# Two hand-overs and the first tiles of layer two: the order of VectorE's splits and of SyncE's loads in a decoder step

## What is computed

```python
def _sq_relu_mlp(x, w1, w2):                 # w1: 1024 x 4096, w2: 4096 x 1024
    return jnp.square(jax.nn.relu(x @ w1)) @ w2
...
for l in range(DEPTH):                       # DEPTH = 2
    ...                                      # l = 0: attention, l = 1: pooling mixer
    xp = xp + _rms(mp, gl[1])
    xp = xp + _rms(_sq_relu_mlp(_rms(xp, gl[2]), mlp_w1[l], mlp_w2[l]), gl[3])
```

## Time and profile before

| | |
|---|---|
| median of three runs | 2125.13 us |
| the profiled execution, its own time | 2128.65 us |
| its span in the profile | 2126.9 us |
| TensorE (PE) busy | 2048.9 us, 96% of the span |
| VectorE (DVE) busy | 1310.8 us, 62% |
| ScalarE (ACT) busy | 922.2 us, 43% |
| GpSimd (POOL) busy | 356.8 us, 17% |
| mean granted TensorE clock | 0.986 of full |

### The profile page before, as it was taken

One profiled execution on the slowest core, in us unless ns is written; L12 is line 12 of the kernel. 1 busy time (PEld: TensorE's weight loads), 2 busy tenths in 40 slices (PEclk: granted clock), 3 DMA queues, 4 the chain that ended last, 5 costly groups with the idle time before them and its releaser, 6 DMA issues.

```text
span 2126.9 us, 34612 instructions
## 1 busy us (share of the span) xinstructions
PE 2048.9 (96%) x13923; PEld 1837.2 (86%) x13923; DVE 1310.8 (62%) x1888; ACT 922.2 (43%) x1591; POOL 356.8 (17%) x375
## 2 busy tenths in 40 slices
PE   7999999999999999999899999989999998999998
PEld 7999877777778899999788878889999997888876
DVE  5121187666556778787645467669687776444475
ACT  5111397645445444444333346454444444333343
POOL 1000131000053333331000013222232320000011
PEclk9999999999999999999999999999999999999999
DMA  5321211099522577777876542444677769664464
GB/s 168 96 74 51 101 70 35 1 355 366 160 97 84 203 260 244 258 246 285 299 252 228 165 159 97 132 135 141 208 256 243 252 223 341 230 223 160 159 221 139
DMA packets 206235, 394.39 MB, mean 185 GB/s; under 512 B 19005, under 2 KB 101109, under 8 KB 197756
## 3 DMA queue, kind: packets, MB, share of 16 engines
q1 hardware_dynamic: 199884, 387.46, 53.4%
q10 hardware_dynamic: 6192, 4.72, 0.7%
HBM read 273.12 MB, written 119.24 MB: 184 GB/s over the span
## 4 chain that ended last, share of the span: by engine, by line
PE 64%; DMA 6%; DVE 5%; POOL 2%; issue 2%; SPq 1%; ACT 1%; POOLq 0%; DVEq 0%; ACTq 0%
PE ps L1957 26%; PE ps L2604 25%; PE ps L4135 4%; PE ps L1975 3%; PE ps L1918 2%; DMA sa_vb_even<-cache_b_v 1%; DMA sa_vb_odd<-cache_b_v 1%; PE ps L4055 1%; DMA l_b_raw<-scratch_t_ops 1%; PE ps L1927 1%; SPq L675 1%; PE ps L4028 1%; DVE l_t_sum L2892 1%; DMA wo_raw<-attn_w_out 1%; DMA l_w_raw<-mlp_w 1%
## 5 line engine op out<-in xcount | busy, mean ns | idle before, releaser
L1957 PE MATMUL ps<-t_b_hi,t_a_hi 128*128 128x512 f32 x448 | 178.2, 398 | 7.3 <-DVE t_b_lo L1751 6.3
L1957 PE MATMUL ps<-l_b_hi,l_a_hi 128*128 128x512 f32 x448 | 175.7, 392 | 8.0 <-DVE l_b_lo L1751 7.0
L1957 PE MATMUL ps<-t_b_lo,t_a_hi 128*128 128x512 f32 x448 | 175.4, 391 | 0.0
L1957 PE MATMUL ps<-t_b_hi,t_a_lo 128*128 128x512 f32 x448 | 175.3, 391 | 0.0
L1957 PE MATMUL ps<-l_b_lo,l_a_hi 128*128 128x512 f32 x448 | 175.2, 391 | 0.0
L1957 PE MATMUL ps<-l_b_hi,l_a_lo 128*128 128x512 f32 x448 | 175.2, 391 | 0.0
L1530 POOL TENSOR_SCALAR stats<-stats 128x1 f32<-128x1 f32 x63 | 32.6, 518 | 785.7 <-ACT t_junk_y L1524 611.0
L1748 DVE TENSOR_TENSOR l_a_lo<-l_a_raw,l_a_hi 128x1024 fp32r<-128x1024 f32 x56 | 68.6, 1225 | 144.3 <-ACT l_a_hi L2634 144.3
L2634 ACT ACTIVATE l_a_hi<-l_a_raw 128x1024 fp32r<-128x1024 f32 x56 | 59.4, 1061 | 219.0 <-PE ps L1975 140.0
L1748 DVE TENSOR_TENSOR t_a_lo<-t_a_raw,t_a_hi 128x1024 fp32r<-128x1024 f32 x56 | 68.6, 1224 | 133.7 <-ACT t_a_hi L2634 133.7
L2634 ACT ACTIVATE t_a_hi<-t_a_raw 128x1024 fp32r<-128x1024 f32 x56 | 59.4, 1061 | 195.8 <-PE ps L1975 135.7
(11 more groups left out here) (390 smaller groups left out, 5693.3 us busy)
## 6 DMA issues: line engine op xcount, KB each, us to landing
scratch_s_ops<-u_s SPq DMA_DIRECT2D x16, 1280.0 KB, 4.8
scratch_t_ops<-u_t SPq DMA_DIRECT2D x16, 1280.0 KB, 5.7
t_a_raw<-scratch_s_ops SPq DMA_DIRECT2D x40, 512.0 KB, 3.9
t_b_raw<-scratch_t_ops SPq DMA_DIRECT2D x40, 512.0 KB, 4.8
scratch_t_ops<-l_t SPq DMA_DIRECT2D x16, 1280.0 KB, 5.5
scratch_s_ops<-l_s SPq DMA_DIRECT2D x16, 1280.0 KB, 4.6
l_a_raw<-scratch_s_ops SPq DMA_DIRECT2D x40, 512.0 KB, 3.9
l_b_raw<-scratch_t_ops SPq DMA_DIRECT2D x40, 512.0 KB, 4.8
```

Of the source, the lines that this page charges most:

```text
L1957: mm = self.nc.tensor.matmul(self.core.ps[:, self.BANK[idx] + tp, :], a[s][:, kk, tp * P:(tp + 1) * P], w[s][:, kk, :], start=(c == 0 and ...
```

## The change

Three edits. In both `up_loads`, `load_operands(3)` is issued before `load_w2(15)` and no longer after it. In `SevenUp.dve_up`, which `LateUp` uses too, VectorE splits operand 2 before `combine_t(15)` and no longer after it, so the loops of both down products start at 3. In `LateUp`, the hand-written orders of VectorE and ScalarE around the direct tiles are changed.

```diff
@@ SevenUp.up_loads
                 self.load_operands(sp, 2)
             if i >= 1:
                 self.store_t(sp, i - 1)
+                if i == PAIRS - 1:
+                    self.load_operands(sp, 3)
                 self.load_w2(sp, i)
-        self.load_operands(sp, 3)
         self.store_s(sp, PAIRS - 1)
         self.store_t(sp, PAIRS - 1)
@@ SevenUp.dve_up
         self.split_operands_lo(dve, 1)
         for piece in range(5):
             self.combine_s(dve, PAIRS - 1, piece)
+        self.split_operands_lo(dve, 2)
         for piece in range(5):
             self.combine_t(dve, PAIRS - 1, piece)
@@ LateUp.act_up
-        order = {1: 2, 2: 4, 3: 3}
+        order = {2: 2, 3: 4, 4: 3}
@@ LateUp.dve_up
         self.token_sum(dve, 1)
+        self.split_lo(dve, 3)
+        self.token_sum(dve, 2)
         for piece in range(5):
             self.combine_t(dve, 0, piece)
-        self.token_sum(dve, 2)
-        self.split_lo(dve, 3)
         self.token_sum(dve, 4)
+        self.split_lo(dve, 4)
         self.token_lo(dve, 2)
-        self.split_lo(dve, 4)
         for piece in range(5):
             self.combine_s(dve, 0, piece)
+        self.split_lo(dve, 5)
+        self.token_sum(dve, 3)
         self.token_lo(dve, 4)
-        self.token_sum(dve, 3)
-        self.split_lo(dve, 5)
         for piece in range(5):
             self.combine_t(dve, 1, piece)
-        self.token_lo(dve, 3)
         for piece in range(5):
             self.combine_s(dve, 1, piece)
         for q in range(4):
             self.w_split_lo(dve, q)
+        self.token_lo(dve, 3)
         self.token_lo(dve, 1)
@@ the down loops of both layers, vector engine
-            for s in range(2, 40):            # layer two: range(2, 56)
+            for s in range(3, 40):            # layer two: range(3, 56)
                 m0.split_operands_lo(dve, s)
```

More of the change, by code:

```diff
@@ L3983, in _ @@
             m1.dve_up(dve)
-            for s in range(2, 56):
+            for s in range(3, 56):
                 m1.split_operands_lo(dve, s)
```

## The result

The changed kernel takes 2132.07 us (median of 20 runs, 2126.06 to 2136.52), the kernel before 2126.1 us in runs on the same chip (20 runs, 2120.72 to 2130.74). The ratio is 1.0029, 95% interval 1.0021 to 1.0037: some 6 us slower, where 3 us faster was predicted. The profiled execution has a span of 2130.9 us instead of 2126.9.

The account below looks back on a forecast made before the run. TensorE, 96% busy, could win only its gaps, 25 us of waits and restarts; 2128.65 - 4.0 + 1.0 = 2125.65 us, and with the median 3.5 us lower, 2122.1 us; range for 8 in 10: 2114 to 2128 us.

Parts of the forecast that it names:

- What bounds the kernel: TensorE's waits at both hand-overs and one direct tile: 16.4 us of waits and 8.4 us of restarts at stake.
- It is not the operand that is late: Both hand-overs: operand 2 is held on VectorE behind combine_t(15), which waits for the last raw weights, landing after 10.65 us.
- Edit 1: Both hand-overs: operand 2 is ready 0.7 us ahead of need, step 2 runs at once, operand 3 is late next.
- Edit 2: Hand-overs: raw weights land 2.6 and 3.3 us later, step 3 waits 3.4 and 4.8 us; gains 2.8 and 2.1 us.
- The first rival: Hand-overs: raw weights hardly delayed, gaining 8.1 us, or 16.6 with no delay; 2118.0 to 2109.5 us; chance 12%.
- Operand 4: Ahead of step 4: load issued later behind store_t(15), costing 0.3 us in layer one and 0.6 in layer two.
- wherever the wait is 3 us or longer: All TensorE waits: a restart at the lower clock costs 2.8 us, charged only from this wait length on.
- The third rival: Hand-overs: operand 4 landing after 11.0 us loses 15.2 us instead of 0.9, giving 2136.4 us; chance 6%.
- Two waits in each hand-over (operand 4): Sign of being wrong in the changed profile: TensorE waits twice per hand-over, because of operand 4.
- Edit 3: Direct tiles of layer two: 5.9 us freed, new 4.3 us wait before the first product, 1.0 us lost overall.
- Sum: Whole kernel: 4.0 us gained at the hand-overs, 1.0 us lost at the direct tiles; median 2122.1 us.

Follow-up runs that it names:

- e3: Kernel before, with only VectorE's split of operand 2 moved ahead of combine_t(15): ratio 1.0002 to the kernel before.
- e1: Kernel before, with operand 3 loaded ahead of the last raw weights and operand 2 split ahead of combine_t(15), direct tiles unchanged: ratio 1.0015 to before.
- e12: Changed kernel, with two loads of pair 4 issued ahead of store_t(1) instead of behind store_s(1): ratio 1.0021 to the kernel before.
- e2: Kernel before, with only the order around the direct tiles of layer two changed: ratio 1.0013 to the kernel before.
- e6: As e1, with operand 3 too split ahead of combine_t(15): ratio 1.0019 to the kernel before.
- e11: As e10, but last raw weights loaded behind operand 4, then operand 5, and combine_t(15) behind operand 4's split: ratio 0.9973 to the kernel before.
- e4: Kernel before, with only operand 3's load moved ahead of the last raw weights: ratio 1.0025 to the kernel before.
- e10: Kernel before, with operand 2 split ahead of combine_t(15), operand 4 loaded ahead of store_t(15), split_lo(3) behind token_sum(1): 2114.44 us, ratio 0.9942.
- e7: As e6, with operands 4 and 5 loaded ahead of store_t(15): ratio 0.9975 to the kernel before.
- e8: Kernel before, with only VectorE's split_lo(3) moved directly behind token_sum(1): ratio 0.9986 to the kernel before.

## Why the prediction was wrong, step by step

**What bounds the kernel.** Right: the waits were found in the right places, and the hand-overs are bound by a full queue of transfers. "It is not the operand that is late" held for operand 2, and I carried it over to operand 4.

**Edit 1.** Right as described: step 2 runs at once, and the wait moves to step 3. Alone it is worth nothing (e3).

**Edit 2.** The delay of the raw weights was right: against operand 2's issue they land 2.9 us later in layer one and 3.7 in layer two (predicted 2.6 and 3.3), and the waits ahead of step 3 are 3.73 and 4.68 us (predicted 3.4 and 4.8). The first rival (weights hardly delayed) is out. But this was also the warning: an edit that puts the raw weights later delays `store_t(15)`, and everything behind it in SyncE's queue.

**Operand 4: the step that failed.** "The wait is 0 if the full queue hides the later issue, 1.3 us if not; I take 0.6. In layer one, by the same steps, it is 0.3." Measured 2.19 and 3.26. There are two errors in it. First the wait itself: b_raw was issued at 1793.38 - 2.5 = 1790.9 on the clock of before (predicted 1790.3); in layer one it took 8.46 us to land instead of the 6.9 of before; and TensorE came to step 4 sooner than I thought, since the restart ahead of step 3 cost 1.9 us and not 2.8. Secondly, I priced a second restart at nothing. In this profile it cost 1.9 us in each layer: from 1029.83 five steps of 5.44 us, 27.2, took 29.10; from 1804.32 they took 29.13 us. I had charged a restart only "wherever the wait is 3 us or longer"; no row showed such a limit, and 2.19 us was enough here.

The hand-overs in these terms, waits and restarts: before 6.3 + 2.9 = 9.2 and 7.0 + 2.8 = 9.8 us, and in the changed kernel 3.73 + 1.9 + 3.26 + 1.9 = 10.8 and 4.68 + 1.9 + 2.19 + 1.9 = 10.7. I had 6.5 and 8.2. The miss of 6.8 us is 5.5 + 3.8 for operand 4's waits and restarts, less 0.9 that I had counted, less 1.8 for cheaper restarts at step 3, and 0.2 at step 3's waits.

Of the two errors only the wait comes back in every profile. e1 and e12 have the same hand-overs, and in them step 4 waits 2.31 and 1.67, 2.23 and 1.82 us, again far more than 0.3 and 0.6. But the restart behind it cost only 0.3 us (27.50 and 27.49, 27.50 and 27.54 us for the five steps), and the one at step 3 cost 3.0 and 2.5, 3.1 and 2.3 us. Their waits and restarts are 9.5 and 8.7, 9.6 and 8.9 us, about what they were before. So the profiles put the hand-overs between even (e1, e12) and 3.3 us lost (the changed kernel), where 4.0 us gained were predicted.

The third rival had this mechanism and the right sign, at 6% and with 2136.4 us. It was too far off: it took a landing of 11.0 us and said that it decides "from a landing of about 9 us on", and the landings were 8.46 and 7.41 us. Its own price of a restart, 2.8 us, put on 1.3 us of wait in each layer as the forecast allowed, would have turned the 4.9 us won in the hand-overs into 3.3 us lost without any longer landing; the forecast left that case out. That the rival's sign came true is in part luck, since edit 3 makes about half of the loss. "Two waits in each hand-over (operand 4)" is what the prediction named as a sign of being wrong, and it is what the profile shows.

**Edit 3.** The mechanism was right, the size short. The wait ahead of tile 3 is gone and there is a new one of 3.96 us ahead of the first product (predicted 4.3), after 17.4 us of VectorE's work (17.5). Tile 5 waited 1.11 us instead of 0.2, since its weights came later and `split_lo(3)` took 2.31 us, while a sum ran on GpSimd, where I had 1.2. The two profiles differ by 1.4 us in the middle (714.0 to 712.6), near my 1.0. But the middle of the kernel before is the longest of six of its order; the means say 2.9 us, and so does e2 (1.0013, 2.8 us, from 0.4 to 5.3). The reason is in the restart that I took as 2.8 us, from the earlier trace rows: in e1, the three tiles after the same wait take 37.82 us (e6: 37.81) instead of the 38.94 there, so their restart was 1.7 us. The gain from removing it was 1.1 us too high.

**Sum.** With edits 1 and 2 at 3.2 us by the runs of e1 (1.1 to 5.5) and edit 3 at 2.8, the change makes the 6 us that were measured. The stretches of the profiles account for less of the first part (hand-overs with edits 1 and 2 in the changed kernel, e1 and e12: mean 59.5 us against 59.0, 1.0 us for both). The remaining 2 us of e1's figure are inside its interval; where they lie, if they are real, stays open. With the mean middle of each order of the tiles (710.8, 713.7 with edit 3, 708.1 with the early split alone), stretches and runs agree within 1.4 us for e2 to e11: e4 5.3 and 5.3, e10 -12.3 and -12.3, e7 -6.1 and -5.3.

## What to carry to other kernels

Where a queue issues loads and stores in program order, look for the first issue that waits for what you have just made later, and list all that stands behind it: here one `store_t` held a load whose data and buffer had been ready for some 8 us, and moving that load past it was worth 12 us where the change had lost 6. Moving work off a late input only pays up to the next consumer that hangs on the same input, so follow the input to its last dependent before adding up. And count each remaining wait with a range for its restart: one wait of 6.3 us cost 9.2 us with it; two of 3.7 and 3.3 us cost 10.8 in the changed kernel, and two of 3.9 and 2.3 us 9.5 in e1.

## What was unexpected of the hardware

The price of a restart of TensorE's clock is not fixed, not even for equal waits. The granted clock in the 5 us after the two waits of layer one, of the changed kernel and of e1 (columns as in the earlier trace rows):

```profile
1019.20:1024.20 5.00, 4.97 (x15) 3.94 (x16) 3.61 (x5) 0.00 (x0) 0.00 (x0) 0.66 0.99 318
1029.80:1034.80 5.00, 4.97 (x15) 3.94 (x16) 3.57 (x4) 2.20 (x4) 0.00 (x0) 0.66 0.74 251
```

```profile
1018.80:1023.80 5.00, 4.95 (x12) 3.89 (x13) 3.63 (x5) 0.00 (x0) 0.00 (x0) 0.50 0.99 312
1029.60:1034.60 5.00, 5.00 (x22) 4.16 (x23) 3.57 (x4) 2.17 (x4) 0.00 (x0) 1.00 0.76 245
```

After 3.73 us and 3.26 us of wait the changed kernel had a mean clock of 0.66 (part of the stretch at 1.2 GHz, part at 2.4), which costs 1.9 us each time. In e1, 3.93 us of wait was followed by 0.50 (1.2 GHz all through, 3.0 us lost), and 2.31 us by 1.00 (2.4 GHz, 0.3 us lost). A wait of 2.19 us cost 1.9 us in the changed kernel and 2.0 in e10, one of 2.59 us in e3 cost 0.3; one of 4.93 us cost 1.6, one of 4.25 us 3.2, one of 9.18 us 2.0. After a single long wait in a hand-over (6.3 to 9.2 us in layer one) it was 1.6 (e4) to 2.9 us (before). So a term of 1 us can't be read from one pair of profiles. Which of the prices a wait gets is not settled here.

The moved `split_lo(3)` took 2.31 us in the changed kernel and in e8, where a sum of weights on GpSimd (3.5 us) runs beside it; the same split of tile 4, with GpSimd idle, took 1.22 us in both. No run takes the GpSimd sum away, so that it is the cause is not shown.
